# Trainium2 decoder trunk in fp32: low-rank products as 64-row pairs, sigmoids in a row, key-norm totals side by side

## What is computed

```python
dx = h_prev - h
xr, xw, xk, xv, xa, xg = (h + dx * mix[i] for i in range(6))
r, k, v = xr @ w_rkvo[0], xk @ w_rkvo[1], xv @ w_rkvo[2]
w_log = -softplus(-(w0 + tanh(xw @ w1) @ w2)) - 0.5        # rank 64
decay = exp(-exp(w_log))
a = sigmoid(a0 + (xa @ a1) @ a2)                            # rank 64
g = sigmoid(xg @ g1) @ g2                                   # rank 160
kk = heads(k * k_k);  kk = kk / max(sqrt(sum(kk * kk, -1)), 1e-12)
k = k * (1 + (a - 1) * k_a)
y = rwkv7_recurrence(heads(r), heads(decay), heads(k), heads(v), -kk, kk * heads(a))
...
y = (group_norm(y) + bonus) * g
return y @ w_rkvo[3]
```

## Time and profile before

| | us |
|---|---|
| median of 3 runs | 1629.69 |
| lowest and highest | 1629.62, 1632.76 |
| profiled execution, its time | 1634.2 |
| profiled execution, its span | 1632.4 |
| TensorE busy | 1504.1 (92% of the span) |
| VectorE busy | 732.3 |
| ScalarE busy | 577.2 |
| GpSimd busy | 598.6 |

### The profile page before, as it was taken

How to read it: one execution, slowest core, us unless ns; L and a number is a source line. 1 busy time by engine, 2 the same in 40 slices (tenths; PEclk the granted TensorE clock), 3 DMA queues, 4 the chain that set the end, 5 groups by cost and what they waited for, 6 DMA issues and landing times. The chain is left out here.

```text
span 1632.4 us, 24876 instructions
## 1 busy us (share of the span) xinstructions
PE 1504.1 (92%) x9769; PEld 1178.7 (72%) x9769; DVE 732.3 (45%) x1133; ACT 577.2 (35%) x887; POOL 598.6 (37%) x325
## 2 busy tenths in 40 slices
PE   4799999666999999999999799979999999999998
PEld 3565677664477888888887577745687888888876
DVE  3883977742735320133135673657544300332143
ACT  4655342333333221222143433248432211222242
POOL 4233331221134344434444234334043444344432
PEclk9898999998999999999999999989999999999999
DMA  4121210003122333232233323120023232322331
GB/s 137 52 77 52 78 52 1 4 5 121 52 78 77 103 103 113 81 103 90 93 109 99 107 79 104 52 78 1 1 78 103 96 108 93 103 96 84 103 103 52
DMA packets 123476, 127.39 MB, mean 78 GB/s; under 512 B 8316, under 2 KB 120060, under 8 KB 123384
## 3 DMA queue, kind: packets, MB, share of 16 engines
q1 hardware_dynamic: 122720, 124.90, 23.4%
q10 hardware_dynamic: 376, 0.61, 0.2%
q0 software_dynamic: 288, 0.59, 0.1%
HBM read 123.96 MB, written 2.12 MB: 77 GB/s over the span
## 5 line engine op out<-in xcount | busy, mean ns | idle before, releaser
L436 POOL TENSOR_TENSOR wlo<-wraw,whi 128x1024 fp32r<-128x1024 f32 x108 | 260.5, 2412 | 834.5 <-ACT whi L1291 793.7
L532 PE MATMUL pb<-xh,whi 128*128 128x512 f32 x1184 | 476.8, 403 | 27.6 <-DVE xl L1800 16.1
L534 PE MATMUL pb<-xh,wlo 128*128 128x512 f32 x1184 | 465.7, 393 | 0.0
L533 PE MATMUL pb<-xl,whi 128*128 128x512 f32 x1184 | 465.6, 393 | 0.0
L532 PEld LDWEIGHTS pb<-xh,whi 128*128 128x128 f32 x1184 | 224.9, 190 | 103.4 <-issue 42.7
L1291 ACT ACTIVATE whi<-wraw 128x2048 fp32r<-128x2048 f32 (+1 forms) x111 | 209.2, 1885 | 232.3 <-PE pb L534 224.6
L439 POOL TENSOR_TENSOR wlo<-wraw,whi 128x1024 fp32r<-128x1024 f32 x111 | 274.2, 2470 | 21.4 <-ACT whi L1291 21.4
L533 PEld LDWEIGHTS pb<-xl,whi 128*128 128x128 f32 x1184 | 225.3, 190 | 47.9 <-issue 3.4
L534 PEld LDWEIGHTS pb<-xh,wlo 128*128 128x128 f32 x1184 | 224.8, 190 | 48.1
L532 PE MATMUL pb<-hid_h,whi 128*128 128x512 f32 x512 | 199.4, 390 | 0.0
L534 PE MATMUL pb<-hid_h,wlo 128*128 128x512 f32 x512 | 199.3, 389 | 0.0
(11 more groups left out here) (267 smaller groups left out, 1755.7 us busy)
## 6 DMA issues: line engine op xcount, KB each, us to landing
wraw<-in_mlp_w_dram SPq DMA_DIRECT2D x128, 512.0 KB, 4.3
wraw<-in_rwkv_w_rkvo_dram SPq DMA_DIRECT2D x32, 512.0 KB, 4.3
wraw<-in_ple_w_gate_dram SPq DMA_DIRECT2D x16, 512.0 KB, 4.3
xtok<-in_x_dram SPq DMA_DIRECT2D x8, 512.0 KB, 6.5
wraw<-in_w_k_shared_dram SPq DMA_DIRECT2D x8, 512.0 KB, 4.4
wraw<-in_w_v_shared_dram SPq DMA_DIRECT2D x8, 512.0 KB, 4.4
wraw<-in_diff_w_q_dram SPq DMA_DIRECT2D x8, 512.0 KB, 3.9
wraw<-in_diff_w_o_dram SPq DMA_DIRECT2D x8, 512.0 KB, 4.4
```

What stands on the lines that cost most here:

```text
L436: pool.tensor_tensor(wlo[:, par, front], wraw[:, par, front], whi[:, par, front].bitcast(F32), ALU.subtract)
L532: mm(o, wh, ah, start=first, stop=False)
L533: mm(o, wh, al, start=False, stop=False)
L534: return mm(o, wl, ah, start=False, stop=last)
```

## The change

- The low-rank second stage: each group g makes the decay tile g and the rate tile g, in pairs of 64-row products, the decay's on rows 0 to 63 into one bank, the rate's on rows 64 to 127 into the other. The zero fills on ScalarE and VectorE go.
- ScalarE: the sixteen sigmoids come in a row, with the weight copy for K-block 0 behind group 2, and the eight high parts of the K input behind all of them, ahead of the weight copy for K-block 1.
- The totals of the key norm: both of a block in one hook, one step later than the first was (two for the pair of R-block 0), and spreads 0 to 2 in one hook at step 7.
- The gate's second part reads rows 96 to 127 only.

```diff
-            pe.wait_ge(s.lora_rdy, 4)
+            pe.wait_ge(s.lora_rdy, 2)
             for g in range(8):
...
-                pair = 1 - g % 2
-                low_rank = (lora_h[:, 0, :], lora_l[:, 0, :]) if g < 4 else (rate_h[:, :], rate_l[:, :])
-                for m in range(2):
-                    c = (2 * g + m) % 8
-                    w = (whi[:, 1, c * P:(c + 1) * P], wlo[:, 1, c * P:(c + 1) * P])
-                    ins = three(pb[2 * pair + m][:, :], 3, w, low_rank, True, True)
+                pair, cols = 1 - g % 2, slice(g * P, (g + 1) * P)
+                dec, rate = slice(0, 64), slice(64, 128)
+                for i, (w, dec_in, rate_in) in enumerate(((whi, lora_h[dec, 0, :], rate_h[rate, :]), (whi, lora_l[dec, 0, :], rate_l[rate, :]),
+                                                          (wlo, lora_h[dec, 0, :], rate_h[rate, :]))):
+                    mm(pb[2 * pair][:, :], w[dec, 1, cols], dec_in, start=i == 0, stop=i == 2)
+                    ins = mm(pb[2 * pair + 1][:, :], w[rate, 1, cols], rate_in, start=i == 0, stop=i == 2)
                 ins.then_inc(s.pe_step, 1)
...
-            hooks = {1: {3: kk_total(0), 4: kk_total(1)}, 2: {3: kk_total(2), 4: kk_total(3)},
-                     3: {3: kk_total(4), 4: kk_total(5)}, 4: {3: kk_total(6), 4: kk_total(7), 5: kk_spread(0), 6: kk_spread(1), 7: kk_spread(2)},
+            hooks = {1: {4: all_of(kk_total, 0, 1)}, 2: {4: all_of(kk_total, 2, 3)}, 3: {4: all_of(kk_total, 4, 5)},
+                     4: {5: all_of(kk_total, 6, 7), 7: all_of(kk_spread, 0, 1, 2)},
                      5: {5: kk_spread(3)}, 6: {6: kk_spread(4), 7: kk_spread(5)}, 7: {1: kk_spread(6)}, 8: {4: kk_spread(7)},
...
-                w = (whi[:, 0, 1024 + c * P:1024 + (c + 1) * P], wlo[:, 0, 1024 + c * P:1024 + (c + 1) * P])
-                three(pb[6 + c % 2][:, :], N_G2, w, (lora_h[:, 2, :], lora_l[:, 2, :]), False, True)\
+                r = slice(96, 128)
+                w = (whi[r, 0, 1024 + c * P:1024 + (c + 1) * P], wlo[r, 0, 1024 + c * P:1024 + (c + 1) * P])
+                three(pb[6 + c % 2][:, :], N_G2, w, (lora_h[r, 2, :], lora_l[r, 2, :]), False, True)\
                     .then_inc(s.pe_step, 1)
...
-            for dst, r, z in ((lora_h[:, 0, :], slice(0, 64), slice(64, 128)), (rate_h[:, :], slice(64, 128), slice(0, 64))):
+            for dst, r in ((lora_h[:, 0, :], slice(0, 64)), (rate_h[:, :], slice(64, 128))):
                 A(dst[r], rstd[r, :], ACT.Copy).then_inc(s.lora_hi, 1)
-                A(dst[z], rstd[z, :], ACT.Copy, scale=0.0).then_inc(s.lora_hi, 1)
...
-            A(lora_h[0:96, 2, :], St[0:96, K_, 1, :], ACT.Copy, scale=0.0).then_inc(s.lora_hi, 1)
             A(lora_h[96:128, 2, :], St[96:128, K_, 1, :], ACT.Copy).then_inc(s.lora_hi, 1)
-            high(4, 0)
 
             for g in range(8):
                 act.wait_ge(s.pe_step, 24 + g + 1)
                 for m in range(2):
-                    c = (2 * g + m) % 8
-                    kind, bias = (LW, V_W0) if g < 4 else (A_, V_A0)
-                    A(St[:, kind, c, :], pb[2 * (1 - g % 2) + m][:, :], ACT.Sigmoid, bias=vec(c, bias))\
+                    kind, bias = (LW, V_W0) if m == 0 else (A_, V_A0)
+                    A(St[:, kind, g, :], pb[2 * (1 - g % 2) + m][:, :], ACT.Sigmoid, bias=vec(g, bias))\
                         .then_inc(s.dense_a, 1)
-                mix_high(3, g, 8 * 2)
+                if g == 2:
+                    high(4, 0)
+            mixes(3, 8 * 2)
             high(5, 1)
...
                 tt(dst[r], src[r], high[r].bitcast(F32), ALU.subtract).then_inc(s.lora_rdy, 1)
-                if z.stop:
-                    ts(dst[z], src[z], 0.0, None, ALU.mult).then_inc(s.lora_rdy, 1)
...
-                dve.wait_ge(s.dense_a, 4 + c + 1)
+                dve.wait_ge(s.dense_a, 4 + 2 * c + 1)
```

More of the change, by code:

```diff
@@ L655, in two_scores, with all_of, g @@
                 return f
-            hooks = {1: {3: kk_total(0), 4: kk_total(1)}, 2: {3: kk_total(2), 4: kk_total(3)},
-                     3: {3: kk_total(4), 4: kk_total(5)}, 4: {3: kk_total(6), 4: kk_total(7), 5: kk_spread(0), 6: kk_spread(1), 7: kk_spread(2)},
+            def all_of(f, *cs):
+                def g():
+                    for c in cs:
+                        f(c)()
+                return g
+            hooks = {1: {4: all_of(kk_total, 0, 1)}, 2: {4: all_of(kk_total, 2, 3)}, 3: {4: all_of(kk_total, 4, 5)},
+                     4: {5: all_of(kk_total, 6, 7), 7: all_of(kk_spread, 0, 1, 2)},
                      5: {5: kk_spread(3)}, 6: {6: kk_spread(4), 7: kk_spread(5)}, 7: {1: kk_spread(6)}, 8: {4: kk_spread(7)},
@@ L1023, in _ @@
             pe.wait_ge(s.w_lo, N_G2 + 1)
-            pe.wait_ge(s.lora_rdy, 7)
+            pe.wait_ge(s.lora_rdy, 4)
             for c in range(CT):
@@ L1821, in lora_low @@
             def lora_low(dst, high, src, r):
-                z = slice(64, 128) if r == slice(0, 64) else slice(0, r.start)
                 tt(dst[r], src[r], high[r].bitcast(F32), ALU.subtract).then_inc(s.lora_rdy, 1)
-                if z.stop:
-                    ts(dst[z], src[z], 0.0, None, ALU.mult).then_inc(s.lora_rdy, 1)
             mixes(0, MIX_W)
@@ L1838, in _ @@
             mixes(2, MIX_G)
-            dve.wait_ge(s.lora_hi, 4)
+            dve.wait_ge(s.lora_hi, 2)
             lora_low(lora_l[:, 0, :], lora_h[:, 0, :], rstd[:, :], slice(0, 64))
             lora_low(rate_l[:, :], rate_h[:, :], rstd[:, :], slice(64, 128))
-            dve.wait_ge(s.lora_hi, 5)
+            dve.wait_ge(s.lora_hi, 3)
             lora_low(lora_l[:, 1, :], lora_h[:, 1, :], St[:, K_, 0, :], slice(0, 128))
-            dve.wait_ge(s.lora_hi, 7)
+            dve.wait_ge(s.lora_hi, 4)
             lora_low(lora_l[:, 2, :], lora_h[:, 2, :], St[:, K_, 1, :], slice(96, 128))
@@ L1852, in log_decays @@
                     dve.wait_ge(s.cst2_in, 16)
-                    dve.wait_ge(s.lora_rdy, 7)
+                    dve.wait_ge(s.lora_rdy, 4)
                     dve.wait_ge(s.pe_step, 8 * N_K)
-                dve.wait_ge(s.dense_a, 4 + c + 1)
+                dve.wait_ge(s.dense_a, 4 + 2 * c + 1)
                 dve.tensor_tensor_scan(St[:, R_, c, :], cst[:, C_SEG:C_SEG + S], St[:, LW, c, :], 0.0, ALU.mult, ALU.add)\
```

## The result

| | before | with the change |
|---|---|---|
| median, us | 1631.07 | 1639.45 |
| lowest and highest, us | 1629.62, 1633.06 | 1635.73, 1640.19 |
| runs | 6 | 6 |
| profiled execution, its time and span, us | 1634.2, 1632.4 | 1639.94, 1638.1 |

The changed kernel is slower: the ratio is 1.0042, with a 95% interval of 1.0030 to 1.0054. The ratio is not the quotient of the medians: 1.0042 is +6.9 us, the medians differ by 8.4. Both medians of the changed kernel, 1639.45 and 1635.88 us, are above the upper end of the forecast range.

The account below looks back on a forecast made before the run. TensorE, busy 92% of the span, was taken to bound the kernel. Terms -7.2 (first spread earlier), -1.4, +0.8 and +2.0 (gate) gave -5.8 us from the profiled 1634.2; against the median, 1623.9 us, range 1617.5 to 1630.5 (forecast's own 1620.5 to 1627.5).

Parts of the forecast that it names:

- Low-rank stage up to K-block 0: Pairs side by side, sigmoids from 76.1 to 87.7 us, K-block 0 starting at 88.9 instead of 91.75, 2.9 us earlier.
- e: Shift of K-block 0's end, and with it of ScalarE's long string of evacuations and squares: 100.9 - 102.7 = -1.8 us.
- Rival 4: Slower by the clock: K-block 0 wholly at half clock, 22 us, ending at 110.9; +5.8, 1635.5 us; chance 8%.
- K-block 1 at 103.4 us: K-block 1 waits for GpSimd behind ScalarE's later weight copy: start 103.4 instead of 102.7 us, 0.7 later.
- Totals in pairs: Key-norm totals: each of four pairs saves TensorE some 1.2 us, three spreads in a row 2.5 us.
- P: Moment of TensorE's first spread product, which releases VectorE's key preparation: 155.2 us instead of 162.39, -7.2 us.
- Behind P: -1.4, +0.8: After the first spread: VectorE's wait for the second root goes, -1.4 us; two spreads may run at half clock, +0.8.
- Rival 2: VectorE takes it back: two more meetings with GpSimd's operations on the string behind P, +4.4, 1628.3 us; chance 17%.
- Gate, +2.0: Output gate: edges between 128-row and 32-row products cost 0.25 us for each of eight c, +2.0 us.

Follow-up runs that it names:

- e2: Kernel before with only the 64-row pairs and the sigmoids in a row (old totals, spreads and gate): 1631.68 us, ratio 0.9994.
- e1: Kernel before with only the paired totals and spreads (old low-rank stage, sigmoids and gate): 1635.34 us, ratio 1.0021.
- e3: Kernel before with only the 32-row second part of the output gate, its needless zero fills gone too: 1634.81 us, ratio 1.0014.
- e7: The changed kernel once more, unaltered, in a later set of runs: 1635.88 us, ratio 1.0029 to the kernel before.
- e4: Changed kernel with the output gate as before (128 rows and zero fills): 1635.41 us, ratio 1.0016 to the kernel before.
- the second set: Later set of runs in which the changed kernel was measured again: 1635.88 us, ratio 1.0029, with the kernel before at 1631.09 us.
- e10: Kernel before with GpSimd's subtraction cut to 32 columns for four weight blocks (most of their low part left out): 1630.18 us, ratio 0.9985.
- e12: Changed kernel, old gate, VectorE's second root inverse one preparation earlier, GpSimd's subtraction for four weight blocks in 512-column instructions: 1628.28 us, ratio 0.9983 to the kernel before.
- e9: Changed kernel, old gate, GpSimd's subtraction cut to 32 columns for four weight blocks: 1624.59 us, ratio 0.9945 to the kernel before.

## Why the prediction was wrong

- **Low-rank stage up to K-block 0: nearly right; e: wrong.** Pairs side by side, sigmoids from 75.92 us (76.1 forecast) to 88.2 (87.7), K-block 0 from 89.71 (88.9). But K-block 0 began at half clock and took 13.6 us where I had allowed 12, so its evacuation began at 103.2, and e was +0.3 instead of -1.8. TensorE had worked ahead of it in short groups with pauses of 0.2 to 1.6 us, and then waited 2.77 us. Rival 4 had the mechanism, with a price far too high: 2.6 us on the block, not 11. (Its own sum has a slip: 110.9 - 102.7 is 8.2, not 8.0.) e2's ratio of 0.9994 says the same: the stage gained nothing.
- **K-block 1 at 103.4 us: right by luck.** It came at 103.35, released by GpSimd. But I had K-block 0 end at 100.9 and TensorE wait 2.5 us for GpSimd. In fact it waited 0.18 us; K-block 0 itself lasted until then.
- **Totals in pairs: right.** P minus e was forecast as -5.4 us and came as -5.0 - 0.3 = -5.3. e1, with the low-rank stage as before, has P 5.1 us earlier. P missed its 155.2 by the error in e.
- **"Behind P: -1.4, +0.8": the step that failed.** I had carried VectorE's string forward unchanged except for its wait. It is not a string of fixed length: moved by 5 us against GpSimd, it had four long meetings instead of one, and 27.6 us instead of 22.7 (24.1 less the wait of 1.4). TensorE waited 8.41 us for it, not 3, and worked 10.8 us at half clock, not the length of two spreads. What I forecast as -0.6 us behind P was +6.1 in the two profiles (P -5.0, inverse +1.05). Other profiles bear this out: from P to the start of the inverse the kernel before, e2 and e3 take 87.7 to 87.8 us, and the four with the paired totals and VectorE's old order (the changed kernel, e7, e4, e1) take 93.8, 92.5, 92.4 and 94.3. Rival 2 was this very mechanism. Its price of two more meetings, +4.4 us, was near the string's +4.9; what I left out was that TensorE, which now came to that point at 181.3 us instead of 190.7, would wait out the whole difference and lose clock on top, so that even its 1628.3 us was 7.6 us below the lower of the two medians. I also gave it 17%, with no reason but that another phase was possible, though the start times of GpSimd's instructions could have been forecast: they follow ScalarE's weight copies, and those were moved in my own working.
- **Gate, +2.0: the edges right, the stage not.** Eight steps of 0.27 are 2.2 us. The rule that I weighed there, that changing the tiling mode drains the engine (the Trainium skill, TensorEngine Tiling (Array Packing), Key Properties), agrees with the trace: 0.33 and 0.32 us at the edges instead of 0.23, while the 64-row pairs start 0.01 us apart. But from the first product of c = 0 to that of c = 7 the changed kernel took 28.15 us (e7 28.21, e3 26.85), where 22.22 and seven edges make 24.1. The rest is half clock, at 432.5 to 442.8 us in the changed kernel, for which I had counted nothing. Whether the 32-row products bring it on is not shown. All three kernels with them have it, but with the old gate five profiles of eleven have some too (23.9 to 25.2 us), e10 among them:

```profile
427.00:433.60 6.60, 5.93 (x13) 3.90 (x14) 2.80 (x4) 1.04 (x2) 0.00 (x0) 0.50 0.00 0
```

- **The whole.** With e = +0.3 and +6.1 behind P, the sum by my own steps would have been 0.3 - 5.3 + 6.1 + 2.2 = +3.3 us. The two profiles differ by 5.7 us: +1.05 at the inverse, +1.6 at the first gate product, +7.65 at the first product behind the gate stage (of the growth in it 2.2 are edges, the rest half clock), and behind it some 2 us come back. The medians differ by more, 8.4 us in the first set, since the profiled execution of the kernel before was 3.1 us above its median and that of the changed kernel only 0.5. In the second set they differ by 4.8. So 5 us or 1.5 us of the medians stand beyond my steps. Stretches of half clock are of that size, and they differ between executions of one kernel (the changed kernel and e7: 10.8 and 5.7 us behind the wait), but no run here isolates them. A profile can also be far from its median: e4's execution, whose inverse started early (248.80), was 4.1 us below.

## What to carry to other kernels

Where a string of VectorE operations is moved in time, lay it against GpSimd's instructions at the new place: each meeting with a two-input operation costs up to the whole GpSimd instruction, and a wait in the old string may have been what hid it. An engine that is made earlier than its partner gains nothing where it next waits for it, and can come out of a long wait at half clock; move the partner's work (here one reciprocal, and shorter GpSimd instructions) together with it. Three products on fewer rows between products on all rows cost their two edges at every place; gathering them in one block would pay the edges once, which was not tried. And a waiting partner's smallest work counts: a copy of zeros of 0.62 us stood ahead of TensorE's wait, and in the one profile of the old low-rank stage without it the half clock behind that wait was gone.

## What the hardware showed that I had not expected

- A VectorE operation with two inputs in SBUF that begins while a GpSimd instruction runs ended, in the changed kernel, 0.3 to 0.6 us behind that instruction's end. It lasted 2.8 to 2.9 us against instructions of 1024 columns, 1.7 to 1.8 against 512 columns, 0.69 alone. TENSOR_SCALAR with one input in SBUF was stopped as well (1.83 instead of 0.54 us), SCALAR_TENSOR_TENSOR with one of its two tensors in PSUM (L1882) and RECIPROCAL were not. GpSimd pays too: its instructions of 2.4 us lasted 2.8 to 2.9 where they began during such an operation.
- Behind TensorE's wait of 8.41 us the products ran at 1.2 GHz, for 10.8 us in the changed kernel and 9.5, 5.7 and 5.6 us in e1, e7 and e4, though they stood one behind the other without a gap. Behind 1.27 us in e12 they ran at 2.4 GHz up to the next wait. The length of the wait alone does not decide it: in e9 a stretch at 1.2 GHz from 183.0 to 189.8 us stands behind a wait of only 1.09 us.
- Two float32 products into different 32-column groups took 1.08 us together, and three 32-row products with 128 columns 1.13 us, hardly more than one alone (1.05 and 1.12). Two fp32r products on 64 rows each started within 0.01 us of each other and took the time of one.
- A 32-row block of three fp32r products cost about 0.1 us at each edge, to the 128-row products ahead and to the transpose behind, another 0.1 us between its first two products, and 0.27 us a step in all.
